# The low parts of the sample chunks: subtracted by GpSimd instead of VectorE

## The reference, cut to what matters

```python
def compress_blocks(x, pe, w1, b1, w2):
    xc = ...reshape(B, nch, CMP_STRIDE, NSA_KV, NSA_HD)      # chunks of 16 rows
    hid = b1
    for r in range(rc):                                       # rc = 2 halves of a block
        hid = hid + jnp.einsum('bcpgd,pdf->bcgf', xc[:, r:r + nb] + pe[r][:, None, :], w1[r])
    return jax.nn.gelu(hid) @ w2
```

## Time and profile before

| what | value |
|---|---|
| time, median of 3 runs | 3484.95 us (3482.47 to 3486.91) |
| the profiled execution's own time | 3489.78 us |
| its span | 3488.0 us |
| PE busy | 3230.7 us, 93% |
| DVE busy | 1371.0 us, 39% |
| ACT busy | 989.5 us, 28% |
| POOL busy | 922.9 us, 26% |
| granted clock of PE, mean | 0.935 |

### The profile page before, as it was taken

One profiled execution on the slowest core, in us unless ns is written; L12 is line 12 of the kernel. 1 busy time (PEld: TensorE's weight loads), 2 busy tenths in 40 slices (PEclk: granted clock), 3 DMA queues, 4 the chain that ended last, 5 costly groups with the idle time before them and its releaser, 6 DMA issues.

```text
span 3488.0 us, 58282 instructions
## 1 busy us (share of the span) xinstructions
PE 3230.7 (93%) x23752; PEld 2946.3 (84%) x23752; DVE 1371.0 (39%) x2939; ACT 989.5 (28%) x1634; POOL 922.9 (26%) x403
## 2 busy tenths in 40 slices
PE   7999998899999999999989999888888887899997
PEld 6999967699998999989987667776677775799997
DVE  3111324411124221241036657766667664411124
ACT  2111210221113211122124444444444443311222
POOL 2333320233334333344220001111111110233332
PEclk9999999999998999989957999899899989899998
DMA  6232221222322223232430004454444544222321
GB/s 140 70 95 73 80 68 52 66 76 70 97 66 76 81 70 97 58 84 70 130 111 1 1 1 152 164 194 160 172 147 156 193 171 120 73 77 80 91 62 35
DMA packets 365938, 329.68 MB, mean 95 GB/s; under 512 B 60469, under 2 KB 345397, under 8 KB 347920
## 3 DMA queue, kind: packets, MB, share of 16 engines
q1 hardware_dynamic: 322264, 180.59, 18.7%
q0 software_dynamic: 21216, 139.89, 11.3%
q10 hardware_dynamic: 22240, 6.17, 0.9%
HBM read 320.39 MB, written 14.58 MB: 96 GB/s over the span
## 4 chain that ended last, share of the span: by engine, by line
PE 79%; issue 8%; DVE 7%; ACT 2%; POOL 1%; DMA 1%; DVEq 0%; POOLq 0%; ACTq 0%
PE psum L1590 51%; PE psum L1854 4%; PE psum L1856 3%; PE psum L1855 3%; PE psum L1910 3%; PE psum L1821 3%; PE psum L2026 2%; PE psum L1943 2%; PE psum L1921 2%; DVE x_lo L1130 1%; PE psum L1874 1%; POOL w_sp L616 1%; PE psum L1584 1%; ACT w_room L913 1%; DMA ring<-in_cache_l_cmp_kv,idxc 1%
## 5 line engine op out<-in xcount | busy, mean ns | idle before, releaser
L1590 PE MATMUL psum<-x_hi,w_sp 128*128 128x288 f32 x5888 | 1042.5, 299 | 38.4 <-DVE x_lo L1130 24.3
L616 POOL TENSOR_TENSOR w_sp<-ring,w_sp 128x2048 fp32r<-128x2048 f32 (+2 forms) x162 | 680.3, 4199 | 1298.9 <-ACT w_sp L759 1298.9
L1590 PEld LDWEIGHTS psum<-x_hi,w_sp 128*128 128x128 f32 x5888 | 880.9, 191 | 43.0 <-issue 23.7
L1590 PE MATMUL psum<-x_lo,w_sp 128*128 128x288 f32 x2944 | 637.5, 299 | 0.0
L1590 PE MATMUL psum<-h_hi,w_sp 128*128 128x288 f32 (+1 forms) x2816 | 502.0, 298 | 0.0
L1590 PEld LDWEIGHTS psum<-x_lo,w_sp 128*128 128x128 f32 x2944 | 481.7, 191 | 0.0
L1590 PEld LDWEIGHTS psum<-h_hi,w_sp 128*128 128x128 f32 (+1 forms) x2816 | 416.5, 188 | 10.5 <-issue 10.1
L1106 DVE TENSOR_TENSOR h_hi<-act_tmp,psum 128x576 f32 (+1 forms) x88 | 66.4, 754 | 861.3 <-ACT act_tmp L798 861.3
L759 ACT ACTIVATE w_sp<-ring 128x2048 fp32r<-128x2048 f32 (+1 forms) x162 | 275.6, 1701 | 445.3 <-PE psum L1590 406.7
L1854 PE MATMUL psum<-ch_hi,w_hi 128*128 128x256 f32 (+1 forms) x1056 | 316.3, 300 | 38.3 <-DVE ch_lo L1263 38.1
L1855 PE MATMUL psum<-ch_lo,w_hi 128*128 128x256 f32 (+1 forms) x1056 | 313.2, 297 | 0.0
(11 more groups left out here) (271 smaller groups left out, 3931.2 us busy)
## 6 DMA issues: line engine op xcount, KB each, us to landing
ring<-in_w_ffn_in SPq DMA_DIRECT2D x168, 512.0 KB
ring<-in_w_ffn_out SPq DMA_DIRECT2D x32, 640.0 KB
ring<-in_w_ffn_out SPq DMA_DIRECT2D x32, 384.0 KB
ring<-in_w_ffn_out SPq DMA_DIRECT2D x32, 320.0 KB
ring<-in_cache_l_win_kv SPq DMA_DIRECT2D x8, 1024.0 KB, 5.5
out<-in_cache_l_win_kv SPq DMA_DIRECT2D x1, 8064.0 KB
ring<-in_w_in_even SPq DMA_DIRECT2D x6, 1024.0 KB
ring<-in_w_in_odd SPq DMA_DIRECT2D x6, 1024.0 KB
```

The lines of the kernel that those rows point to most:

```text
L616: pool.tensor_tensor(w_sp[:, u % 2, 1, 0:w], ring[:, slot, 0:w], w_sp[:, u % 2, 0, 0:w].bitcast(F32), ALU.subtract).then_inc(lo_ready, 1)
L1590: last = pe.matmul(out[:, c], lhsT, rhs[:, c * TH:(c + 1) * TH], start=start, stop=stop)
```

## The change

The low parts of the sample chunks are subtracted by POOL instead of DVE. POOL's list of work in the loop is written anew, so that the subtractions stand between the gathers. A new semaphore, `ch_low_pool`, tells PE.

```diff
+        ch_low_pool = sem("ch_low_pool")
...
+            def load_in(b, load):
+
+                slot_read(b, load)
+                c = load - WIN_LOAD
+                if load < WIN_LOAD:
+                    gather(load, cmp_rows, idxc[:, b * 8 + load:b * 8 + load + 1])
+                elif load > WIN_LOAD:
+                    gather(load, slc_rows, idx[:, (c - 1) % 4, 2 * b + (c - 1) // 4:2 * b + (c - 1) // 4 + 1])
+
+            for load in range(6):
+                load_in(0, load)
             for b in range(DB):
-                for load in range(8):
-                    slot_read(b, load)
-                    gather(load, cmp_rows, idxc[:, b * 8 + load:b * 8 + load + 1])
-                for c in range(1, 9):
-                    slot_read(b, WIN_LOAD + c)
-                    gather(WIN_LOAD + c, slc_rows, idx[:, (c - 1) % 4, 2 * b + (c - 1) // 4:2 * b + (c - 1) // 4 + 1])
+                for i in range(XS):
+                    pool.wait_ge(ch_high, b * XS + XP + i + 1)
+                    pool.tensor_tensor(ch_lo[:, i % 4], ch_raw[:, i % 4], ch_hi[:, i % 4].bitcast(F32), ALU.subtract)\
+                        .then_inc(ch_low_pool, 1)
+                    if i % 8 == 7:
+                        load_in(b, i // 8 * 2 + 6)
+                        load_in(b, i // 8 * 2 + 7)
+                for load in (14, 15, 16):
+                    load_in(b, load)
+                if b + 1 < DB:
+                    for load in range(6):
+                        load_in(b + 1, load)
...
                 for i in range(XS + 1):
                     if 4 <= i < XS:
                         turn(b, o, i)
-                    if i > 0:
-                        low_phase(b * XS + (o * XS + XP + i - 1), (i - 1) % 4, 64)
                     if i == 4 and o == 1:
                         merge_weights(b)
...
                 for i in range(XS):
-                    pe.wait_ge(ch_low, b * XS + (o * XS + XP + i + 1))
+                    pe.wait_ge(ch_low_pool, b * XS + (o * XS + i + 1))
```

## The result

The kernel after takes 3549.89 us, median of 4 runs (3537.32 to 3557.2); the kernel before, beside it, 3483.78 (3482.47 to 3486.91). The ratio is 1.0185, 95% interval 1.0152 to 1.0217: slower by about 66 us. The forecast was 3510 with a range of 3495 to 3541. The sign was right and the size was not: 24.8 us were foreseen. The profiled execution took 3537.32 us, with a span of 3535.5 and a mean granted clock of 0.929.

What follows compares the result with a forecast made beforehand. PE, busy for 93% of the span, was taken to set the pace. The terms +11.6 - 0.3 + 4.0 + 9.5 = +24.8 us, on the median of 3484.95, gave 3509.8, predicted as 3510, range 3495 to 3541.

Steps and rivals of the forecast that it cites:

- Term 1: PE's start of phase 0 in seven samples: the first subtraction stands behind loads 4 and 5, +11.6 us.
- Sample 0's -0.3: Start of sample 0: its gathers are long issued and POOL need not wait for DVE's four turns, about -0.3 us.
- The price of a subtraction: One 512-column subtraction on POOL: 1.25 us taken, range 1.21 to 1.55, against 0.65 on DVE.
- Term 2: Merge and two gathers behind it, seven samples: PE's wait moves to phase 7, gathers delay phase 8, +4.0 us.
- Term 3: Two gathers within steady work: PE waits 1.05 us at phase 24 and sample 0's phase 8, nine times, +9.5 us.
- What costs nothing: DVE's lost subtractions, 159 us of work, mostly lie under PE's phases; gathers that move later cause no counted wait.
- POOL becomes the bound: Rival in the compress: subtractions of 1.36 to 1.55 us make POOL late, 3524 to 3560; chance of 1.4 or more 0.2.
- Faster: Rival: subtractions run beside the gathers' issue, so phases 0 and 8 start sooner, -16 us, 3469; chance 0.04.
- no change: Rival: PE's waits were set by turns and merge, never by the subtraction; within 7 us of before, chance 0.04.
- Only the start costs: Rival: gathers inside the compress hold POOL less or slack is larger, 3490, or 3500 with term 3 alone gone; chance 0.15.

Runs made afterwards that it cites:

- e_first: Changed kernel with the first subtraction of samples 1 to 7 ahead of loads 4 and 5 instead of behind them; 3545.2 us, ratio 1.0180.
- c_best_mw: Changed kernel with early subtractions 0 and 1, gathers one by one, loads 12 and 13 late, merge in four pieces, merge_weights ahead of turn 4; 3495.5 us, ratio 1.0041.
- b_dummy: Kernel before, with two unused 128x512 subtractions added on POOL beside merge; 3497.1 us, ratio 1.0037.

## Why the prediction was wrong, step by step

- **Term 1, the start: right.** +11.6 us foreseen for the seven samples, +11.9 measured, and each sample's own figure within 0.1 us; POOL goes load 4, load 5, subtraction without a gap. Sample 0's -0.3 lies ahead of the measured stretch, and the traces show it: PE idles 3.42 us before that phase instead of 3.75.
- **The price of a subtraction: right within its bounds.** 1.25 us taken, 1.29 measured, 1.24 from start to start in a row. A wait on each adds nothing where it is already met. POOL's busy time grew by 316 us (320 foreseen). DVE's fell by 135 and not by 165: 8 us of the difference are the held time, which the page counts as busy. The subtractions that went had 167 us between their own starts and ends, but part of that lay under the instruction ahead or behind (in the earlier trace rows the turn that starts at 2192.22 ends at 2192.93, and the low part behind it starts at 2192.86), which the page counts once.
- **Term 2, "takes 4.29 us as before": this step failed.** The wait moved to phase 7, and phase 7 took 3.73 us until phase 8, both as foreseen. But merge took 5.61: 1.32 us in seven samples, 9.2 us. The forecast had looked at the very mechanism, sized it at 2.4 us from the one long instruction (L1537, now L1553), and left it out. That instruction was never held. It began at 2197.20, after POOL's subtractions were through, since the small ones ahead of it had been held: each ended just behind the end of a subtraction, whatever its own size. That the two exclude each other is the rule of the Trainium skill, "SBUF — State Buffer", section "Who interferes with whom", which the prediction named; the trace agrees (0.16 against 0.72 us in the same line), and the test beside the kernel before agrees (4.29 against 5.74 us). The error was to look for it in the long instruction alone; left out of the sum, it was worth four times what it was sized at. The phases 5 to 7 grew by 13.3 us where 4.0 were foreseen; the difference is this hold.
- **Term 2, phases after it at full clock: failed.** The forecast named the low clock as what would make it wrong, 1.7 us for each 3.4 us at 0.50, and gave it no place in the sum. The gap before phase 7 is 3.4 us instead of 2.2; phases 8 and 9 then took 2.72 and 2.5 to 2.6 us in five of the seven samples, at a granted clock of 0.50: +12.1 us. That the idle time ahead brings the low clock is shown by the products that kept PE at work (20.5 before, 32.6 after, 21.0 with them). The trace of before had already shown the lower level behind a gap of 2.67 us. Whether one of 2.2 us, as foreseen, would have kept the full clock was not tried.
- **Term 3, two gathers in steady work: right in kind, small.** Phase 24 starts 1.1 us late, as worked out, and the phase behind it takes 0.1 us more. Phase 16, "just hidden", starts up to 0.3 us late, which with the phase behind it is +2.7 us: its cover was 0.2 us thick. With sample 0's two waits the measured sum is 8.3 + 2.4 + 2.7 = 13.4 against 9.5.
- **"What costs nothing": failed for loads 12 and 13.** They were counted among gathers that "move later" and are read much later. That is true of their data. But they were moved closer to the loop's step, from 4.8 to 3.1 us ahead of it, and the step is longer the more of their transfer lies in it (2.3 to 2.6 us with none): +10.6 us. The forecast asked only who reads a load, and not what its transfer lies beside. The step is an idle time of DVE that the trace of before already showed to vary, 3.1 to 4.4 us.
- **Rivals.** "POOL becomes the bound" gave times in the right region (3524 to 3560), but by a subtraction above 1.36 us, which it is not; its mechanism did not occur. "Faster" and "no change" did not either. "Only the start costs" is refuted by phases 7 and 24.

In sum: 11.9 (start) + 25.4 (phases 5 to 9: 4.0 foreseen, 9.2 hold, 12.1 clock) + 13.4 + 10.6 (step) + 1.5 (the rest) = 62.7 us, but for rounding. The missing 38 us are the hold (9.2), the clock (12.1), the step (10.6), 4 us of term 3 and 2 us of small rests.

## What to carry to other kernels

When elementwise work moves from VectorE to GpSimd, list every VectorE instruction with two SBUF inputs that can fall beside it, the tiny ones first: each can be held to the end of a GpSimd instruction or of a whole row of them, and what counts is what is queued behind it. When work is put between DMA issues, follow each transfer to its new place in time and ask what else uses DMA there, an engine's step around a loop included. Where a gap of TensorE grows, price the phases behind it at both levels of the clock.

## What the runs showed of the hardware

- A VectorE instruction of 128x8 took 3.56 us (e_first), one of 128x11 2.48 (c_best_mw), each held until 0.03 to 0.04 us behind the end of a row of GpSimd subtractions of 128x512, which follow at 1.24 us. In these cases it did not get in between two of them. In others it did: in the kernel after, where the second subtraction waited for its high part (a pause of 0.13 us, 2.71 less twice 1.29), and also with no pause at all, as in e_first, where the 128x2 instruction of 2199.81 ended at 2200.57, 0.02 us behind the first of two subtractions that together took 2.50 us. What decides between the two was not found.
- A pair of TENSOR_SCALAR instructions of 128x9 whose scalar is read from SBUF took 1.42 us beside GpSimd's subtractions (b_dummy) and 0.49 without (c_best_mw, behind the row).
- The first instruction of VectorE after the branch of a loop came 2.3 to 2.6 us after the last one with idle DMA engines, and 4.9 to 6.0 us when two gathers of 1 MB each had been issued 4.3 and 3.1 us before that last one ended. In all kernels it came 1.9 to 2.2 us after the start of an instruction packet of 8 KB, and the growth lay ahead of that packet.
- A GpSimd gather takes 0.94 us and 0.30 between two of them, but a subtraction follows a gather with no gap (2204.06 + 0.94 to 2205.02).
